# Expert up weights fetched with two neighbouring rows per partition (8 KB runs), and the spread reading every sixteenth column to match

## The reference

```
h = rmsnorm(x, norm2_g)                       # 288 x 2048, the gain is per column
group = argmax over 4; two experts of its 4 per token, weights from a softmax
for e in range(16):
    gate, up = split(h @ expert_w_up[e])      # 2048 x 1024
    out += combine[:, e] * ((silu(gate) * up) @ expert_w_down[e])   # 512 x 2048
y = rmsnorm(x + out, final_norm_g)
```

## Time and profile before

| | us |
|---|---|
| median of 3 runs | 1740.81 |
| profiled execution | 1743.25 |
| its span | 1741.1 |
| TensorE busy | 1696.4 (97%) |
| TensorE weight loads busy | 1335.0 (77%) |
| VectorE busy | 718.8 (41%) |
| ScalarE busy | 662.2 (38%) |

### The profile page before, as it was taken

How to read it: one execution, slowest core, us unless ns; L and a number is a source line. 1 busy time by engine, 2 the same in 40 slices (tenths; PEclk the granted TensorE clock), 3 DMA queues, 4 the chain that set the end, 5 groups by cost and what they waited for, 6 DMA issues and landing times. The chain is left out here.

```text
span 1741.1 us, 27405 instructions
## 1 busy us (share of the span) xinstructions
PE 1696.4 (97%) x10644; PEld 1335.0 (77%) x10644; DVE 718.8 (41%) x1058; ACT 662.2 (38%) x1112; POOL 127.8 (7%) x176
## 2 busy tenths in 40 slices
PE   5999999999999999999999999999999999999997
PEld 4999999999999999999999999998433333333332
DVE  5888885444444554455444545544000100100101
ACT  6666664333344444444433334545011121121101
POOL 1545440000000000000000000000000000000000
PEclk9999999999999999999999999999999999999999
DMA  8466555666765565565776566472999999999993
GB/s 208 132 168 162 154 151 145 180 158 168 198 168 140 161 184 148 139 168 158 163 179 177 148 181 172 128 241 92 388 378 380 414 382 381 411 376 380 413 413 158
DMA packets 418885, 393.50 MB, mean 226 GB/s; under 512 B 19168, under 2 KB 376896, under 8 KB 409664
## 3 DMA queue, kind: packets, MB, share of 16 engines
q1 hardware_dynamic: 407152, 383.04, 69.0%
q10 hardware_dynamic: 10432, 4.79, 1.1%
q0 software_dynamic: 1232, 4.72, 1.0%
HBM read 385.38 MB, written 11.08 MB: 228 GB/s over the span
## 5 line engine op out<-in xcount | busy, mean ns | idle before, releaser
L1109 PE MATMUL bank<-hH,wH 128*128 128x288 f32 x1792 | 537.3, 300 | 5.7 <-ACTq L732 2.7
L1539 DVE TENSOR_TENSOR wL<-ring,wH 128x1024 fp32r<-128x1024 f32 x320 | 388.1, 1230 | 354.1 <-ACT wH L669 346.3
L669 ACT ACTIVATE wH<-ring 128x1024 fp32r<-128x1024 f32 x320 | 335.9, 1058 | 520.2 <-PE bank L1111 454.3
L1110 PE MATMUL bank<-hL,wH 128*128 128x288 f32 x1792 | 529.7, 296 | 0.0
L1111 PE MATMUL bank<-hH,wL 128*128 128x288 f32 x1792 | 529.5, 295 | 0.0
L1109 PEld LDWEIGHTS bank<-hH,wH 128*128 128x128 f32 x1792 | 338.5, 189 | 12.7 <-issue 6.6
L1110 PEld LDWEIGHTS bank<-hL,wH 128*128 128x128 f32 x1792 | 338.3, 189 | 0.4
L1111 PEld LDWEIGHTS bank<-hH,wL 128*128 128x128 f32 x1792 | 337.9, 189 | 0.0
L1343 PE MATMUL bank<-raw,hgs 128*64 128x512 f32 x1024 | 236.5, 600 | 0.0
L1336 PE MATMUL bank<-raw,atA 128*96 128x512 f32 x512 | 231.9, 597 | 0.0
L1343 PEld LDWEIGHTS bank<-raw,hgs 128*64 128x64 f32 x1024 | 66.8, 136 | 147.2 <-issue 145.7
(11 more groups left out here) (307 smaller groups left out, 1484.9 us busy)
## 6 DMA issues: line engine op xcount, KB each, us to landing
raw<-in_expert_w_up SPq DMA_DIRECT2D x128, 1024.0 KB, 9.1
ring<-in_w_in SPq DMA_DIRECT2D x112, 1024.0 KB, 6.7
raw<-in_expert_w_down SPq DMA_DIRECT2D x64, 1024.0 KB, 8.4
ring<-in_w_pb SPq DMA_DIRECT2D x16, 1024.0 KB, 9.1
ring<-in_w_pa SPq DMA_DIRECT2D x16, 1024.0 KB, 9.2
ring<-in_w_o SPq DMA_DIRECT2D x16, 1024.0 KB, 5.9
cK<-in_cache_k SPq DMA_DIRECT2D x16, 256.0 KB, 2.8
cV<-in_cache_v SPq DMA_DIRECT2D x16, 256.0 KB, 3.3
```

The source lines that it names most:

```text
L669: a.activation(wH[2 * (slot % 2) + half][:, :, :], ring[slot][:, 8 * half:8 * half + 8, :], ACT.Copy).then_inc(hi_ready, 1)
L1109: pe.matmul(dst, hi, rH[:, k, :], start=(k == 0), stop=False)
L1110: pe.matmul(dst, hi, rL[:, k, :], start=False, stop=False)
L1539: v.tensor_tensor(lo[:, :, :], ring[slot][:, 8 * half:8 * half + 8, :], hi[:, :, :].bitcast(F32), ALU.subtract).then_inc(lo_ready, 1)
```

## The change

The rows of an expert's up matrix are dealt out in another order. Before, row k * 128 + p belongs to partition p; now row p * 16 + k does. Piece s holds k = 2s and 2s + 1, which for a partition are two neighbouring rows: one run of 8 KB. The runs of two neighbouring partitions start 64 KB apart. So that channels and rows match, `spread` takes the columns k, k + 16, k + 32, ... as weights for k instead of 128 neighbours, and the gain is fetched once more in the same order (`gup`), by a transfer of its own of 64 bytes per partition; ScalarE and VectorE wait for it once. The router still uses `g2`.

```diff
+    gup = sb("gup", [P, KT])
...
-    up_v = expert_w_up[0].rearrange("e (k p) n -> p e k n", p=P)
+    up_v = expert_w_up[0].rearrange("e (p k) n -> p e k n", k=KT)
...
+            sp.dma_start(gup[:, :], norm2_g[0].rearrange("(p k) -> p k", k=KT)).then_inc(gup_in, 16)
...
                     ins = a.activation(hgs[:, q // ROUNDS % 2, k, :, :].rearrange("p e s -> p (e s)"),
-                                       round_banks(q)[0][:, 256 * c:256 * (c + 1)], ACT.Copy, scale=g2[:, k:k + 1])
+                                       round_banks(q)[0][:, 256 * c:256 * (c + 1)], ACT.Copy, scale=gup[:, k:k + 1])
...
+            a.wait_ge(gup_in, 16)
             for q in range(7):
                 drain(q)
...
                 for x in (xsH, xsL):
-                    ins = pe.matmul(dst.rearrange("p (e s) -> p e s", e=EPG), x[:, k * P:(k + 1) * P], R[:, :, 0, :],
+                    ins = pe.matmul(dst.rearrange("p (e s) -> p e s", e=EPG), x[:, k::KT], R[:, :, 0, :],
                                     start=(x is xsH), stop=(x is xsL), skip_group_check=True)
...
-                                g2[:, k:k + 2].rearrange("p (k a) -> p k a", a=1).to_broadcast([P, 2, EPG * ES]),
+                                gup[:, k:k + 2].rearrange("p (k a) -> p k a", a=1).to_broadcast([P, 2, EPG * ES]),
...
             one_hots(0)
+            v.wait_ge(gup_in, 16)
             v.wait_ge(cnt_ps, 1)
```

More of the change, by code:

```diff
@@ L356, in build @@
         trio = [bank[0:2], bank[2:4], bank[4:6]]
+        gup_in = sem("gup_in")
         x_in = [sem(f"x_in{f}") for f in range(FT)]
@@ L1042, in again @@
                                 a.activation(hgs[:, 0, k, :, :].rearrange("p e s -> p (e s)"),
-                                             bank[4 + k % 4][:, 0:EPG * ES], ACT.Copy, scale=g2[:, k:k + 1])\
+                                             bank[4 + k % 4][:, 0:EPG * ES], ACT.Copy, scale=gup[:, k:k + 1])\
                                  .then_inc(ovhg_out, 1)
```

## The result

The changed kernel takes 1755.97 us (median of 6 runs, 1754.14 to 1758.48) against 1740.82 for the kernel before on the same chip (6 runs, 1739.58 to 1741.33): a ratio of 1.009 [1.0077, 1.0102]. It is slower by 0.9%, where I had forecast 1742.0 and no change. Its profiled execution took 1758.46 us, 15.2 more than that of before, over a span of 1756.4.

The account below looks back on a forecast made before the run. The prediction took TensorE's own work as the bound, with no piece late. Its terms 0 + 0 + 0.9 + 0.3 made 1.2 us, which carried over to the median of 1740.81 gave 1742.0; range 1739.5 to 1756.0.

Parts of the forecast that it names:

- What bounds the kernel: Expert stage: TensorE runs at its own pace, every fetch waits for it and none makes it wait.
- Fetch: Up fetches in 8 KB runs: any saving lands while a piece already lies ready, so 0 us.
- place of the rows: Up pieces' partitions 64 KB apart in HBM: taken as 0 us, since runs are 8 KB like the down piece's.
- The gain's own load: Extra small fetch ahead of the first weight tile: 0.1 to 0.5 us, taken as 0.3.
- the sign that I had named: For the extra gain fetch: ScalarE's first split of a tile would start at 19.0 to 19.4 us.
- Spread: Strided weight loads of 128 spread products in the expert stage: 0 to 2 us in all, taken as 0.9.
- The bound from VectorE: Upper bound for the spread's loads: a wide step doubles a read, as in VectorE's copies, giving 13.3 us.
- A: Slower rival: strided load exposed, spread interval 0.118 to about 0.222 us; 1754.4 us, or 1760.6 at the dearer read; chance 0.33.
- B: Slower rival: scattered HBM rows starve TensorE once up fetches are 12% slower; 1763 us at 20%; chance 0.05.
- C: Faster rival: larger packets shorten the expert stage by 6 to 9 us, to 1733; chance 0.05.
- D: Rival: up fetch unchanged in effect, packets stay 4 KB or larger ones no faster; same time as the forecast; chance 0.04.
- a rule: Trainium skill on SBUF: 16-byte lines, another line at each access penalised; applied to the spread's load, 13.3 us.

Follow-up runs that it names:

- experiment 9: Kernel before, and the same with the new fetch alone, both with second-half products cut to 64 columns: 1708.78 us with 4 KB packets, 1700.04 with 8 KB.
- e1_fetch: Changed kernel with the spread on 128 neighbouring columns again, so only the fetch is new: 1742.91 us, ratio 1.0005 to the kernel before.
- e2_stride: Changed kernel with the old up fetch of two 4 KB runs per partition, spread still strided: 1756.92 us, ratio 1.0088 to the kernel before.
- Experiment 5: Kernel before plus 84 products and transposes that nothing reads, their operands read at various steps from 1 to 32 elements: 1757.35 us in a single run.
- e3_pairs: Kernel before with partition p taking rows 2p and 2p+1 of each 256-row block, spread on every second column, gain matched: 1743.59 us, ratio 1.0009.

## Why the prediction was wrong

**What bounds the kernel: right.** TensorE's own work set the end before and after; from the first up product on TensorE waited for no piece in any profile but the light pair's of experiment 9, and the one gain of the fetch lay in landing times.

**Fetch and place of the rows, 0 and 0: right.** `e1_fetch` moved the stretch of the pieces by 0.02 us. Its price, had it been exposed, is shown by the pair of experiment 9: a gain of 8.7 us, not a loss. I had bounded the 64 KB pitch by the first weight tiles' 290 GB/s; experiment 9 read at 421. By the Trainium skill (DMA: Bandwidth & Descriptors, Latency and other measured facts) it should have lost 3% or less, and no loss is seen at all. Of the two nearest rows the piece of equal run length was the right one.

**The gain's own load, 0.3: not confirmed.** The extra issue is there (7.55 to 8.02 us), and the first weight tile is issued 0.35 us later than in the earlier trace rows. But the sign that I had named did not come: ScalarE's first split starts at 18.61 us, not at 19.0 to 19.4, and so earlier than the 18.91 of the earlier trace rows, and TensorE's first product of a weight tile starts at 22.54 against 22.85 before. In `e1_fetch` and `e2_stride`, with the same load, it starts at 22.78 and 23.25. The 0.3 us by which the changed kernel is behind at 28 us come only when TensorE's pace doubles, at 27.9 us in the one trace and at 26.9 in the other. The 0.16 us at the stage's beginning are within what one execution differs from another, so no run shows a price of this load.

**Spread, 0.9: wrong, and this is the step that failed.** It says that the transposes' loads show "the read side can deliver a column in 0.47 ns, and what holds the spread's loads at 0.81 is something else", so that a doubled read would be 120 ns and nearly disappear under the product's 116. In place of that the interval went from 118 to 224 ns, 128 x 0.106 = 13.6 us. The error is to treat the fastest read of another form as a floor that is common to all forms, and the rest as a fixed time beside it, of which a stride touches nothing. Experiment 5 shows both halves: the transposes' load does go from 0.47 to 0.9 or 1.0 ns a column, and the product's load, with the same operand and the same steps, pays another 1.0 to 1.2 on its 0.81. The row that was nearest in kind for the read (32 bits, 128 columns) was far off in what sets the price. The bound from VectorE, that a wide step doubles whatever the read takes, gave 13.3 us and was right to 0.3, in part by luck. It rested on 4 ns between VectorE copies of 5 and of 3 elements, and it took the longer load from 104 ns, though by the prediction's own words a load costs something only beyond some 110: that gives 128 x (0.208 - 0.110) = 12.5 us. The load was then dearer than doubled: 224 ns for 128 columns are 1.75 ns a column, 2.2 times 0.81. The two errors cancel.

**The clock, 1.6: not foreseen.** No term of the sum stood for it, and no sentence gave a reason to put it at nothing. The first group's stretch is the one where TensorE comes out of waits, and the longer loads there were followed by 6.83 us at half clock.

**The rivals.** A, 1754.4 at a chance of 0.33, happened by its own mechanism and at its own place: 13.6 against the 13.3 of its price, and with the 1.6 of clock the measured 1755.97 instead of 1754.4. That 1755.97 still lies in the range, by 0.03 us, says nothing for the forecast: the range was drawn up to 1756.0 to take A in. B and C were tested by `e1_fetch` and by experiment 9 and fell; D fell too, since the packets did change. The chances were the second fault: a rule and VectorE's rows stood together for A, and against them one inference of mine that no strided read of TensorE supported.

## What to carry to other kernels

On a path that TensorE bounds, leave the columns of a product's weights adjacent or at most two 32-bit elements apart; here a step of 16 bytes or more doubled the load's interval (118 to 224 ns for 128 columns), and nothing hid it where load and product were of one length. If a layout in HBM asks for larger packets, choose one that pairs neighbours within a block: `e3_pairs` has the same 8 KB packets at a ratio of 1.0009. And before paying for a faster transfer, find the stretch in which a transfer ends a wait: here none did, so the best of these kernels only equalled the one before.

## What the runs showed of the hardware that I had not expected

- A product's weight load is nearly free at a step of 8 bytes (195 ns for 188), half-priced at 12 (260) and full-priced from 16 (333), while the moving operand and the loads of 32-bit transposes pay in full at 8 already (interval 227 for 119; load 209 for 139).
- A step of 16 elements is cheaper than one of 8: 315 against 340 ns, and 222 against 243 ns in the interval.
- A load of 128 columns starts beside products with weights of 96 columns, but not beside pairs of products with 64: 0.11 against 0.55 us for the same spread.
- Loads at a step of 16 in the first group came with half the clock for 6.83 us in each of four profiles; with steps of 1 or 2 at that place it stayed whole in all eight others. What links the two stays open.
